# Two row norms moved behind their projections, and a residual updated by column halves, in a two-block transformer kernel

## The reference

```python
h = h + rms_norm(y, g_mix_post[l])                  # y: sliding-window attention and HGRN, times w_out
u = rms_norm(h, g_x_pre[l])
m = rms_norm(mem, g_mem[l])
y = cross_attention(u, m, wq_x[l], wk_x[l], wv_x[l], wo_x[l])     # 4 heads of 256, 256 keys
h = h + rms_norm(y, g_x_post[l])
u = rms_norm(h, g_ffn_pre[l])
y = (jax.nn.silu(u @ w_gate[l]) * (u @ w_up[l])) @ w_down[l]      # 2816 wide
h = h + rms_norm(y, g_ffn_post[l])
```

## Time and profile before

| | |
|---|---|
| median of three runs | 946.61 us (942.06 to 949.55) |
| profiled execution, its time | 948.43 us |
| its span | 946.6 us |
| mean granted clock of TensorE | 0.952 |
| TensorE matmul busy | 861.0 us, 91% |
| VectorE busy | 602.7 us, 64% |
| ScalarE busy | 461.2 us, 49% |
| GpSimd busy | 13.9 us, 1% |

### The profile page before, as it was taken

How to read it: one execution, slowest core, us unless ns; L and a number is a source line. 1 busy time by engine, 2 the same in 40 slices (tenths; PEclk the granted TensorE clock), 3 DMA queues, 4 the chain that set the end, 5 groups by cost and what they waited for, 6 DMA issues and landing times. The chain is left out here.

```text
span 946.6 us, 13559 instructions
## 1 busy us (share of the span) xinstructions
PE 861.0 (91%) x5329; PEld 759.9 (80%) x5329; DVE 602.7 (64%) x923; ACT 461.2 (49%) x717; POOL 13.9 (1%) x20
## 2 busy tenths in 40 slices
PE   3789798989999999999998989899899599999996
PEld 2587586867889999998788967668877599999885
DVE  3678976569667888885557666635645655555543
ACT  4835245145546666664445565425444454444442
POOL 0001000000000000000000000000000000000000
PEclk9799799999799999999999999879899799999998
DMA  9775665006655666655557544105423256665551
GB/s 321 237 267 179 244 195 151 23 24 213 186 175 181 179 182 187 186 180 189 171 152 250 170 134 136 52 28 173 156 89 110 70 178 184 188 185 181 194 159 44
DMA packets 103507, 153.95 MB, mean 163 GB/s; under 512 B 6504, under 2 KB 55700, under 8 KB 103444
## 3 DMA queue, kind: packets, MB, share of 16 engines
q1 hardware_dynamic: 100320, 144.60, 48.9%
q10 hardware_dynamic: 3124, 8.49, 2.4%
HBM read 152.01 MB, written 1.05 MB: 162 GB/s over the span
## 5 line engine op out<-in xcount | busy, mean ns | idle before, releaser
L1728 DVE TENSOR_TENSOR w_lo<-raw,w_hi 128x1024 fp32r<-128x1024 f32 (+1 forms) x244 | 294.2, 1214 | 210.9 <-ACT w_hi L1246 210.6
L1246 ACT ACTIVATE w_hi<-raw 128x1024 fp32r<-128x1024 f32 (+1 forms) x244 | 254.3, 1049 | 257.2 <-PE bank L677 128.5
L751 PE MATMUL bank<-hT_hi,w_hi 128*128 128x256 f32 x864 | 247.2, 286 | 9.4 <-DVE hT_lo L1789 6.5
L752 PE MATMUL bank<-hT_lo,w_hi 128*128 128x256 f32 x864 | 246.4, 285 | 0.0
L753 PE MATMUL bank<-hT_hi,w_lo 128*128 128x256 f32 x864 | 246.4, 285 | 0.0
L751 PEld LDWEIGHTS bank<-hT_hi,w_hi 128*128 128x128 f32 x864 | 168.0, 194 | 10.7 <-issue 9.5
L752 PEld LDWEIGHTS bank<-hT_lo,w_hi 128*128 128x128 f32 x864 | 168.1, 195 | 0.0
L753 PEld LDWEIGHTS bank<-hT_hi,w_lo 128*128 128x128 f32 x864 | 167.8, 194 | 0.0
L675 PE MATMUL bank<-w_hi,hT_hi 128*128 128x512 f32 (+2 forms) x224 | 88.0, 393 | 12.9 <-DVE w_lo L1728 7.6
L676 PE MATMUL bank<-w_lo,hT_hi 128*128 128x512 f32 (+2 forms) x224 | 86.4, 386 | 0.0
L677 PE MATMUL bank<-w_hi,hT_lo 128*128 128x512 f32 (+2 forms) x224 | 86.1, 384 | 0.0
(11 more groups left out here) (314 smaller groups left out, 1195.0 us busy)
## 6 DMA issues: line engine op xcount, KB each, us to landing
raw<-w_up_dram SPq DMA_DIRECT2D x132, 256.0 KB, 3.4
raw<-w_ada_dram SPq DMA_DIRECT2D x48, 512.0 KB, 4.8
raw<-w_down_dram SPq DMA_DIRECT2D x44, 512.0 KB, 3.5
raw<-w_in_dram SPq DMA_DIRECT2D x40, 512.0 KB, 4.5
raw<-w_gate_dram SPq DMA_DIRECT2D x44, 256.0 KB, 2.9
raw<-w_out_dram SPq DMA_DIRECT2D x16, 512.0 KB, 3.7
raw<-wk_x_dram SPq DMA_DIRECT2D x8, 512.0 KB, 3.6
raw<-wv_x_dram SPq DMA_DIRECT2D x8, 512.0 KB, 3.4
```

Source lines behind the costliest of these rows:

```text
L751: pe.matmul(o, hi[:, c:c + P], xh[:, k, :], start=f, stop=False, skip_group_check=True)
L752: pe.matmul(o, hi[:, c:c + P], xl[:, k, :], start=False, stop=False, skip_group_check=True)
L1246: act.activation(unit_view(w_hi[n % NSPLIT], u), unit_view(raw[u % NRAW], u), ACT.Copy).then_inc(w_hi_ready, 1)
L1728: dve.tensor_tensor(unit_view(w_lo[n % NSPLIT], u), unit_view(raw[u % NRAW], u), unit_view(w_hi[n % NSPLIT], u).bitcast(F32), ALU.subtract ...
```

## The change

In the cross attention and in the feed-forward of the second block the input is turned without its row factor: `turn` reads `res` itself instead of `row` (names `xpre` and `ffnpre` are now `UNSCALED`), and the squares of `res`, the variance and the power are computed while the projection runs. In the attention the factor enters where scores are scaled: the constant scale becomes a column of 128 values, 1/16 times the row factor, for the exponential and, negative, for the maximum. In the feed-forward the output has tokens in the free dimension, so the factor is spread: VectorE makes the identity times the factor (`diag`), TensorE multiplies it by ones (`r2` in PSUM, behind the third unit of `gu0`), VectorE copies it, and then multiplies both halves of each panel by it out of PSUM into `conv`; `silu` and the product now read `conv`.

`postnorm` updates `res` in four pieces, column half p outermost and tile t inside it. `turn` on TensorE waits for each half alone. For the attention, `wv1` is interrupted: two units, pairs 0 and 1 of the turn (in banks 6 and 7), one unit, pairs 2 and 3, one unit. On VectorE `postnorm` no longer calls `feed` for its second panel but `feed_units` up to that panel's own end, and behind the last gain product it splits the first two units of the panel `ahead`, where it split all of `wv1` before; for the feed-forward `ahead` is now `gu0`, where there was none. `turn` has no `after` any more in the attention, so it feeds no unit between its pairs; `feed("wv1")` follows it. The result is stored in four pieces, two issued by SP and two by ScalarE.

```diff
             def turn(name, wait_src=None, pairs=None, banks=None):
...
-                    o = claim(use, next_small())
+                    o = claim(use, banks[p % len(banks)] if banks else next_small())
+                    if name in UNSCALED:
+                        pe.wait_ge(res_ready, RES[BEFORE[name]] - 2 * T + T * (p // 2 + 1))
...
             def ffn(up, down, pre, gen):
                 turn(pre)
-                for p in range(NFF):
-                    cols_panel(f"{up}{p}", hT_hi, hT_lo, turn_before(pre) if p == 0 else None)
+                first = cols_steps(f"{up}0", hT_hi, hT_lo, turn_before(pre))
+                if pre in UNSCALED:
+                    for _ in range(3):
+                        next(first)
+                    use = ("r2",)
+                    o = claim(use, next_small())
+                    pe.wait_ge(diag_ready, T)
+                    for t in range(T):
+                        ins = pe.matmul(o[:, t * P:(t + 1) * P], ones, diag[:, t * P:(t + 1) * P], start=True, stop=True)
+                    fill(ins, use)
+                run(first)
+                for p in range(1, NFF):
+                    cols_panel(f"{up}{p}", hT_hi, hT_lo)
...
-            rows_panel("wv1", memT_hi, memT_lo, b=4)
-            turn("xpre")
+            wv1 = rows_steps("wv1", memT_hi, memT_lo, b=4)
+            next(wv1)
+            next(wv1)
+            turn("xpre", None, range(2), (6, 7))
+            next(wv1)
+            turn("xpre", None, range(2, 4), (6, 7))
+            run(wv1)
...
-            for t in range(T):
-                sp.wait_ge(res_ready, RES["ffnpost"] - (T - 1 - t))
-                sp.dma_start(out[0, t * P:(t + 1) * P, :], res[:, t, :]).then_inc(stored, 16)
+            for p in range(2):
+                sp.wait_ge(res_ready, RES["ffnpost"] - 2 * T + T * p + 1)
+                sp.dma_start(out[0, 0:P, 512 * p:512 * p + 512], res[:, 0, 512 * p:512 * p + 512]).then_inc(stored, 16)
...
                     ins = act.activation(prob_of(i)[:, 0:n], src, ACT.Exp, bias=nmax[:, i, 1:2],
+                                         scale=xscale[:, 0, t:t + 1] if kind == "x" else scale,
...
             square_out("wout2_", "mixpost")
             feed_units(last_unit["wv1"] + 1)
+            turn("xpre")
+            feed("wv1")
             square_res("xpre", "mixpost")
             copy_row("wv1", Vx[:, :, 512:])
-            turn("xpre", "wv1")
-            feed("wv1")
             for p in range(2):
                 feed(f"wq{p}")
...
+            act.wait_ge(xscale_ready, 2)
             attend("x")
             turn("xo")
             square_out("wo", "xpost")
+            turn("ffnpre")
+            feed_units(first_unit["gu0"] + NSPLIT)
             square_res("ffnpre", "xpost")
-            turn("ffnpre")
             for p in range(NFF):
                 feed(f"gu{p}")
-                use = (f"gu{p}", 0)
-                ready(act, use)
+                emptied(act, (f"gu{p}", 0))
                 if p >= 2:
-                    emptied(act, (f"gu{p - 2}", 1))
-                free(act.activation(sg[:, p % 2, :, :], ps(use)[:, :].rearrange("p (k t) -> p k t", k=2),
-                                    ACT.Silu), use)
-                emptied(act, (f"gu{p}", 1))
+                    act.wait_ge(prod_ready, NFF + p - 1)
+                act.activation(sg[:, p % 2, :, :], conv[:, p % 2, 0, :, :], ACT.Silu).then_inc(sg_ready, 1)
+                act.wait_ge(prod_ready, NFF + p + 1)
                 act.activation(act_hi[:, 2 * p:2 * p + 2, :], prod[:, p % 2, :, :], ACT.Copy).then_inc(act_hi_ready, 1)
...
-                for p in range(2):
-                    feed(f"{panel_name}{p}")
-                    for t in range(T - p):
-                        times_gain(p, t)
+                feed(f"{panel_name}0")
+                for t in range(T):
+                    times_gain(0, t)
+                feed_units(last_unit[f"{panel_name}1"] + 1)
+                times_gain(1, 0)
                 variance(name)
                 times_gain(1, 1)
                 if ahead:
-                    feed_units(last_unit[ahead] + 1)
+                    feed_units(first_unit[ahead] + 2)
                 dve.wait_ge(rstd_ready, POW[name] + 1)
-                for t in range(T):
-                    for p in range(2):
+                for p in range(2):
+                    c = slice(512 * p, 512 * p + 512)
+                    for t in range(T):
                         emptied(dve, (f"{panel_name}{p}", t))
-                    dve.scalar_tensor_tensor(res[:, t, :], row[:, t, :], rstd[:, POW[name], t:t + 1], res[:, t, :],
-                                             ALU.mult, ALU.add).then_inc(res_ready, 1)
+                        dve.scalar_tensor_tensor(res[:, t, c], row[:, t, c], rstd[:, POW[name], t:t + 1],
+                                                 res[:, t, c], ALU.mult, ALU.add).then_inc(res_ready, 1)
...
             postnorm("mixpost", "wout2_", 0, "wv1")
-            prenorm("xpre", "mixpost")
+            feed_units(last_unit["wv1"] + 1)
+            turn("xpre")
+            feed("wv1")
             copy_row("wv1", Vx[:, :, 512:])
-            turn("xpre", "wv1")
-            feed("wv1")
-            for p in range(2):
-                feed(f"wq{p}")
+            feed("wq0")
+            variance("xpre")
+            feed("wq1")
+            dve.wait_ge(rstd_ready, POW["xpre"] + 1)
+            dve.tensor_scalar(xscale[:, 0, :], rstd[:, POW["xpre"], 0:T], X_SCALE, None, ALU.mult).then_inc(xscale_ready, 1)
+            dve.tensor_scalar(xscale[:, 1, :], rstd[:, POW["xpre"], 0:T], -X_SCALE, None, ALU.mult).then_inc(xscale_ready, 1)
+            dve.wait_ge(xscale_ready, 2)
             attend("x")
             turn("xo")
-            postnorm("xpost", "wo", 1)
-            prenorm("ffnpre", "xpost")
+            postnorm("xpost", "wo", 1, "gu0")
             turn("ffnpre")
+            feed_units(first_unit["gu0"] + NSPLIT)
+            variance("ffnpre")
+            dve.wait_ge(rstd_ready, POW["ffnpre"] + 1)
+            for t in range(T):
+                dve.tensor_scalar(diag[:, t * P:(t + 1) * P], ident, rstd[:, POW["ffnpre"], t:t + 1], None,
+                                  ALU.mult).then_inc(diag_ready, 1)
+            feed("gu0")
+            ready(dve, ("r2",))
+            free(dve.tensor_copy(r2[:, :], ps(("r2",))[:, 0:TOK]), ("r2",))
+            emptied(dve, ("r2",))
+
+            def times_r2(p, half):
+
+                use = (f"gu{p}", half)
+                ready(dve, use)
+                ins = dve.tensor_tensor(conv[:, p % 2, half, :, :], ps(use)[:, :].rearrange("p (k t) -> p k t", k=2),
+                                        r2[:, :].unsqueeze(1).broadcast_to([P, 2, TOK]), ALU.mult)
+                free(ins, use)
+
             for p in range(NFF):
                 feed(f"gu{p}")
-                use = (f"gu{p}", 1)
-                ready(dve, use)
-                emptied(dve, (f"gu{p}", 0))
-                free(dve.tensor_tensor(prod[:, p % 2, :, :], ps(use)[:, :].rearrange("p (k t) -> p k t", k=2),
-                                       sg[:, p % 2, :, :], ALU.mult), use)
+                times_r2(p, 0)
+                times_r2(p, 1)
+                emptied(dve, (f"gu{p}", 1))
+                dve.wait_ge(sg_ready, NFF + p + 1)
+                dve.tensor_tensor(prod[:, p % 2, :, :], conv[:, p % 2, 1, :, :], sg[:, p % 2, :, :],
+                                  ALU.mult).then_inc(prod_ready, 1)
```

More of the change, by code:

```diff
@@ L224, in key_tiles @@
     return {"mla": 4, "swa": t + 1, "x": 2}[kind]
+UNSCALED = ("xpre", "ffnpre")
 MLA_PANELS = (6, 7, 8, 9)
@@ L316, in build @@
         sums = sb("sums", [P, 8])
-        rs12 = sb("rs12", [P, T])
+        scales = sb("scales", [P, 3, T])
+        rs12, xscale = scales[:, 0, :], scales[:, 1:3, :]
         modc = sb("modc", [P, 6 * 8])
@@ L330, in build @@
         epoch = at[0]
+        at[0] = prob_at
+        diag = sb("diag", [P, TOK])
+        r2 = sb("r2", [P, TOK])
         at[0] = prob_at
@@ L499, in build @@
         sg_ready = sem("sg_ready")
+        diag_ready = sem("diag_ready")
+        xscale_ready = sem("xscale_ready")
         prod_ready = sem("prod_ready")
@@ L599, in square_column @@
             return ssq[:, c:c + 1]
-        TURN_SRC = {"ctx": lambda t, k: in_ctx[:, t, k * P:(k + 1) * P],
+        TURN_SRC = {"xpre": lambda t, k: res[:, t, k * P:(k + 1) * P],
+                    "ffnpre": lambda t, k: res[:, t, k * P:(k + 1) * P],
+                    "ctx": lambda t, k: in_ctx[:, t, k * P:(k + 1) * P],
                     "mix": lambda t, k: mix_row[:, t, k * P:(k + 1) * P],
@@ L628, in turn_gain @@
             return vec(gain, k), None
[L632 removed]
+        NORM_ROWS = ["ctx", "x1", "cq", "ckv", "ckvc", "mem", "x2", "mix"]
         ROWS_BY_DVE = {name: sum(T if WIDTH.get(m, D) == 256 else 1 for m in NORM_ROWS[:n + 1])
@@ L757, in cols_steps, with turn @@
```

(21 more changed lines are left out.)

9 lines of the change are left out of this document (7 added, 2 removed).

## The result

The changed kernel takes 950.81 us (median of seven runs, 949.92 to 952.77) against 946.61 us before: ratio 1.006, 95% interval 1.0036 to 1.0085. That is slower by 3 to 8 us, where 1.5 us was forecast; the time lies in the range given, 942.5 to 954.5 us. The profiled execution took 949.92 us, with a span of 948.1 us. Against the 946.6 us of before this says little: the stretch up to the end of `wout2_1`, which nobody changed, took 649.95 us before and 646.04 us after, and between 646.0 and 650.9 us in all the profiles that follow.

| us behind the end of `wout2_1` | before | after |
|---|---|---|
| first `wv1` matmul | 0.00 | 4.93 |
| first transpose for the queries | 11.18 | 11.99 |
| first `wq0` matmul | 16.20 | 21.75 |
| first score matmul of the attention | 41.95 | 46.35 |
| first matmul on the probabilities | 46.27 | 51.95 |

A forecast was written before the change was run, and what follows sets the result against it. TensorE was taken as the bound in nearly all of the second half. Terms +3.5 + 0.3 - 2.3 + 0 = +1.5 us gave 949.9 us on the profiled execution and 948.1 us against the median 946.61; range 942.5 to 954.5 us.

The forecast's parts named there:

- The stall ahead of `wv1`: Between `wout2_1` and `wv1`: TensorE newly idles 4.9 us, because VectorE splits the first two units behind the last gain product.
- The clock after it: Early in `wv1`: the new idling drops the granted clock to 0.50, losing 2.0 to 3.0 us, taken as 2.5.
- The wait ahead of `wq0`: Between `wv1` and `wq0`: TensorE waits 2.1 us (670.2 to 672.3) for the low part of the weight split.
- the clock falls twice: Rival: the 2.1 us before `wq0` cost the clock again, +2.5 us, giving 950.6 us; chance 0.13.
- what goes: Third attention's input: 3.1 us idling, 2.6 us lost at low clock and 0.3 us before the transposes, 6.0 us removable.
- Forecast +3.5: Third attention's input, up to `wq0`: 4.9 + 2.5 + 2.1 - 6.0 us.
- The attention itself: Third attention's start: scale columns, their wait and slower exponentials cost +0.3 us, between 0 and 0.7.
- The column's own price: Attention's exponentials: each grows by 0.09 us with a column as scale; first and last on the path, 0.2 us.
- The feed-forward: From the norm behind `wo1` into `gu0`: earlier start less low clock and r2 matmuls, -2.3 us, between -1.2 and -3.3.
- The loop: Feed-forward's eleven panels: two more VectorE products each only cut slack from 2.5 to 1.1 us; cost 0.
- The end: Last residual pieces and result transfers: smaller last piece changes 0 us, between -0.4 and +0.2.

The follow-up runs named there:

- experiment 2: Changed kernel with VectorE splitting the next panel's first two units ahead of the last gain products: 942.95 us, ratio 0.9981 to the kernel before.
- experiment 3: Changed kernel with dummy matmuls ahead of `wv1`, `wq0` and the first matmul on the probabilities: 945.5 us, ratio 1.0024 to the kernel before.
- experiment 5: Changed kernel without ScalarE's own wait for the scale columns ahead of the attention: 947.44 us, ratio 1.003 to the kernel before.
- experiment 6: Kernel before with only one more wait, for a long-ready value, ahead of the cross attention's first exponential: 945.72 us, ratio 1.0004 to the kernel before.
- experiment 1: Changed kernel run once more unaltered (also called the repetition): 951.15 us, ratio 1.0068 to the kernel before.
- experiments 6 and 4: The second of the pair: changed kernel with scale columns made ahead of VectorE's last three weight splits before the attention; 951.21 us, ratio 1.0078 to the kernel before.

## Why the prediction was right, and where its sum was off

The time lies in the range, and the direction and the stalls ahead of `wv1` and `wq0` came as described. The sum did not: +1.5 us was forecast for what measured 4.2 to 6.5 us, and one step failed, the attention.

*The stall ahead of `wv1`* (4.9 us forecast) was 4.93, with the cause given; experiment 2 shows it.

*The clock after it* (2.5 us, between 0 and 3.0) was 1.5 us by experiment 3. *The wait ahead of `wq0`* (2.1) was 2.3. But behind it the clock fell again, 1.5 us: that is the rival "the clock falls twice", to which I gave 0.13, with 2.5 us as its price. Its time, 950.6 us, is nearly the 950.81 us measured, but by luck: the second fall is 1.5 us of it, and the attention supplies the rest. For what goes, 6.0 us, the six profiles of kernels with that wait of 3.1 to 3.2 us, the one before among them, say that 2.6 us of it are lost in four of six executions. Forecast +3.5, measured +4.4.

*The attention itself* is the step that failed: +0.3 us, between 0 and 0.7, measured +3.1. I asked whether the load stays ahead of the new wait and priced its being held back at 0.45 us, because I let it wait for the columns alone. It waits for the maximum, which makes the load (1.28 us) and the maximum a chain instead of neighbours: 1.2 us (from the first score to the first matmul on the probabilities 5.60 us, and 4.40 without the third wait). I also held that the clock bears this stretch's gaps, since before it had stayed at 1.00; at 2.5 us it fell, 1.7 us more. Experiments 5 and 6 show the load, experiment 3 the clock; experiment 5 removes both together. The column's own price held: the exponential takes 0.56 us instead of 0.47. The Trainium skill (ScalarE: Activation LUTs, What ACT_TABLE_LOAD costs) gives about 93 ns for each pointer operand, which agrees; its load of 1283 ns agrees too, while the drain that it adds is not seen here.

*The feed-forward* (-2.3, between -3.3 and -1.2): `gu0` came 2.8 us earlier against the end of `wo1` (11.10 instead of 13.93), and up to the end of `dn1` 0.2 to 1.15 us went back: -1.7 to -2.6. Where the clock was at 1.00 before `gu0` began, `gu0` to the end of `dn1` took 188.80 us (experiment 1) against 188.36 with the old loop (experiment 6), so the new products cost 0.4 us, as forecast; the rest is how long the clock stayed low. *The loop* cost nothing: no wait in eleven panels, though each chain grew by 1.46 us. VectorE's busy time grew by 13.2 us, where I expected some 15. *The end* gave 0.43 us where I took 0 and bounded it at 0.4.

The sum of +1.5 us was 5.4 us in the profile and 4.2 us between the medians, 6.5 us in the repetition. Of the 3.9 us by which the profile exceeds the sum, the attention is 2.8 us, its input 0.9 and the feed-forward 0.6, less 0.4 at the end. The range was also not what its parts add up to: bounds of -4.8 and +6.2 us around 946.61 with 3 us for the median on either side make 938.8 to 955.8 us, not 942.5 to 954.5; the measured time lies in both.

## What to carry to other kernels

When a wait is added ahead of an activation that loads a table, look in the compiled program at which waits now stand ahead of the load: here a third wait moved the one that mattered, whatever it waited for. Work that needs nothing of a norm, such as a weight split for the next panel, belongs ahead of the wait for that norm on its engine; a change that moves a norm away must be read for the places where its idle time was being used. And an idle gap of 2 to 3 us on TensorE has two prices, with and without the clock; put both into the range.

## What the runs showed of the hardware

The clock fell behind gaps of 2.3 us ahead of `wq0` in four profiles of five with that wait (not in that of experiment 2), behind 2.3 to 2.5 us ahead of the probabilities in four of four, and not behind 2.1 us in experiment 6. Behind 3.1 us it fell in four of six; two kernels were profiled twice, and each showed both. Behind 4.8 us and more, ahead of `wv1` and in the feed-forward, it fell each time. So between 2.3 and 3.1 us no length of a gap decides it alone here. The Trainium skill (TensorE: Matmul & The Clock Gate, What's actually happening) says that the gate's window runs freely and does not start with the kernel; two profiles of one kernel that differ behind the same 3.08 us fit this, and nothing here tests it further. Once it had fallen, it took 1.5 to 1.7 us behind the gaps of 2.3 to 4.9 us and 2.6 us behind that of 3.1 us.

A table load with only the bank's wait ahead of it follows the evacuation by 0.02 us, and the exponential follows the load by 0.01 us (experiment 5); with the maximum's wait ahead of it too, ScalarE idles for 0.88 to 1.21 us first (experiments 6 and 4, and the change).
